# Inputs laid out by feature and weight unit, and a new order for the first eight units

## The reference

```python
def rmsnorm(x, g):
    xf = x.astype(jnp.float32)
    y = xf * lax.rsqrt(jnp.mean(xf * xf, axis=-1, keepdims=True) + EPS)
    return (y * g.astype(jnp.float32)).astype(x.dtype)
...
    for l in range(DEPTH):
        h = rmsnorm(x, norm_mix[l])
        y, S, b = mixer(h, S_in[l], buf_in[l], start_pos, lbs[l], w_in[l], w_o[l], hg_norm[l], pool_w[l], pool_scale[l])
        x = x + y
        h = rmsnorm(x, norm_ffn[l])
        if l % 2 == 0:
            x = x + swiglu(h, ffn_w_gate[j], ffn_w_up[j], ffn_w_down[j])
        else:
            x = x + moe(h, router[j], moe_w_gate[j], moe_w_up[j], moe_w_down[j])
```

## Time and profile before

| | |
|---|---|
| median of 3 runs | 991.08 us (989.86, 991.08, 997.3) |
| the profiled execution | 987.79 us, its span 986.0 us |
| mean granted TensorE clock | 0.971 |
| TensorE / VectorE / ScalarE / GpSimd busy | 93% / 71% / 58% / 17% |

### The profile page before, as it was taken

How to read it: one execution, slowest core, us unless ns; L and a number is a source line. 1 busy time by engine, 2 the same in 40 slices (tenths; PEclk the granted TensorE clock), 3 DMA queues, 4 the chain that set the end, 5 groups by cost and what they waited for, 6 DMA issues and landing times.

```text
span 986.0 us, 15383 instructions
## 1 busy us (share of the span) xinstructions
PE 917.2 (93%) x5943; PEld 843.2 (86%) x5943; DVE 697.8 (71%) x814; ACT 574.6 (58%) x711; POOL 170.3 (17%) x146
## 2 busy tenths in 40 slices
PE   0698999999999999989996999999999999999996
PEld 0598989999999999989886897888888888888886
DVE  0579947466665554797546568898989889898953
ACT  0555447554444335644544476878786868787842
POOL 0207405621121211273071000000000000000000
PEclk9999979999999999999896799999999999999999
DMA  9374303596569854632025458999999999899911
GB/s 267 89 214 129 108 1 106 150 250 186 174 200 284 217 150 135 172 113 73 28 92 172 147 176 321 414 389 352 368 366 349 376 343 394 328 407 318 394 40 45
DMA packets 171186, 217.82 MB, mean 221 GB/s; under 512 B 6908, under 2 KB 141244, under 8 KB 170986
## 3 DMA queue, kind: packets, MB, share of 16 engines
q1 hardware_dynamic: 163293, 206.25, 62.0%
q10 hardware_dynamic: 6461, 5.54, 1.9%
q0 software_dynamic: 1376, 5.27, 1.8%
HBM read 210.06 MB, written 7.43 MB: 221 GB/s over the span
## 4 chain that ended last, share of the span: by engine, by line
PE 80%; DVE 6%; ACT 3%; issue 3%; POOL 3%; DMA 3%; ACTq 2%; DVEq 0%; SPq 0%; POOLq 0%
PE bank L1565 37%; PE bank L1295 9%; PE bank L1296 9%; PE bank L1297 9%; PE bank L1539 3%; PE bank L1324 2%; PE bank L1435 2%; PE bank L1365 2%; PE bank L1614 2%; DMA sb_raw<-in_ffn_w_up_dram 1%; POOL at_state L468 1%; ACTq L501 1%; ACT sb_w_hi L512 1%; DVE at_sided L948 1%; PE bank L1574 1%
## 5 line engine op out<-in xcount | busy, mean ns | idle before, releaser
L861 DVE TENSOR_TENSOR sb_w_lo<-sb_raw,sb_w_hi 128x1024 fp32r<-128x1024 f32 (+1 forms) x116 | 163.5, 1412 | 81.0 <-ACT sb_w_hi L512 78.8
L512 ACT ACTIVATE sb_w_hi<-sb_raw 128x1024 fp32r<-128x1024 f32 (+1 forms) x116 | 126.9, 1100 | 135.3 <-PE bank L1297 116.9
L1295 PE MATMUL bank<-at_act_hi,sb_w_hi 128*128 128x264 f32 x672 | 193.9, 288 | 10.8 <-DVE sb_w_lo L861 8.1
L1565 PE MATMUL bank<-sb_w_hi,at_packed 128*128 128x512 f32 (+1 forms) x768 | 192.6, 380 | 3.0 <-DVE sb_w_lo L1073 1.6
L1296 PE MATMUL bank<-at_act_lo,sb_w_hi 128*128 128x264 f32 x672 | 191.4, 285 | 0.0
L1297 PE MATMUL bank<-at_act_hi,sb_w_lo 128*128 128x264 f32 x672 | 191.3, 285 | 0.0
L1073 DVE TENSOR_TENSOR sb_w_lo<-at_raw_e,sb_w_hi 128x1408 fp32r<-128x1408 f32 (+1 forms) x112 | 159.2, 1448 | 29.0 <-ACT sb_w_hi L723 28.9
L1073 DVE TENSOR_TENSOR sb_w_lo<-sb_raw,sb_w_hi 128x1408 fp32r<-128x1408 f32 (+1 forms) x104 | 149.9, 1472 | 21.1 <-ACT sb_w_hi L723 20.4
L1565 PEld LDWEIGHTS bank<-sb_w_hi,at_packed 128*128 128x128 f32 x768 | 141.4, 190 | 27.1 <-DVE at_packed L1087 1.7
L723 ACT ACTIVATE sb_w_hi<-at_raw_e 128x1408 fp32r<-128x1408 f32 (+1 forms) x112 | 139.4, 1245 | 42.8 <-PE bank L1565 37.2
L723 ACT ACTIVATE sb_w_hi<-sb_raw 128x1408 fp32r<-128x1408 f32 (+1 forms) x104 | 130.5, 1262 | 37.5 <-PE bank L1565 35.7
(11 more groups left out here) (258 smaller groups left out, 1428.3 us busy)
## 6 DMA issues: line engine op xcount, KB each, us to landing
sb_raw<-in_moe_w_up_dram SPq DMA_DIRECT2D x36, 704.0 KB, 7.3
at_raw_e<-in_moe_w_down_dram SPq DMA_DIRECT2D x49, 512.0 KB, 6.6
at_raw_e<-in_moe_w_gate_dram SPq DMA_DIRECT2D x35, 704.0 KB, 8.6
sb_raw<-in_w_in_dram SPq DMA_DIRECT2D x40, 512.0 KB, 4.0
sb_raw<-in_moe_w_gate_dram SPq DMA_DIRECT2D x29, 704.0 KB, 8.8
sb_raw<-in_moe_w_down_dram SPq DMA_DIRECT2D x39, 512.0 KB, 4.7
at_raw_e<-in_moe_w_up_dram SPq DMA_DIRECT2D x28, 704.0 KB, 6.0
sb_raw<-in_ffn_w_gate_dram SPq DMA_DIRECT2D x22, 512.0 KB, 4.0
```

The source lines that it names most:

```text
L512: act.activation(w_hi[s][:, 0:kts, :], raw[s][:, 0:kts, :], ACT.Copy).then_inc(hi_done, 1)
L861: dve.tensor_tensor(w_lo[s][:, 0:kts, :], raw[s][:, 0:kts, :], w_hi[s][:, 0:kts, :].bitcast(f32), ALU.subtract).then_inc(lo_done, 1)
L1295: pe.matmul(out[:, 0:T], w_hi[s][:, k, :], hi[:, c, :], start=(c == 0), stop=False)
L1565: mm = pe.matmul(bank[first_bank + p][:, 0:width], s, w[:, c0:c0 + width], start=(k == 0 and n == 0), stop=(k == last and n == 2))
```

## The change

- The inputs are rearranged before the launch (no arithmetic): x by feature, the vectors as one table of 128 rows, every dense weight by unit so that a unit is one contiguous block with 4 KB (down: 5.6 KB) per partition; state, pool map and router likewise, and the recurrent states are stored by feature and turned back afterwards. The expert weights stay as they are.
- Start: SP loads x in four pieces of two tiles, then units 1, 2, 3 (the constants between), units 4 to 7, and then the state, tables, past rows, pool map and router. ACT issues only the vector table and unit 0. No transposes.
- ACT and DVE: two tiles of x, unit 0's split, the other six tiles, units 1 and 2. TensorE's unit 0 waits per tile of `act_lo`.
- Squares on ACT (four, two tiles each), POOL adds them up to one tile in four adds, TensorE does one ones matmul after unit 2, into bank 7. The copy of the pooling state to its output is issued by POOL after these adds.
- Units 4 to 7 of `in0` use banks 4 to 7, so the first eight units wait for no read. ACT takes the root after split 4, then the lower bounds' Exp; DVE reads units 0 to 2 at step (0,2), and makes the lower bounds after the read of unit 3.

The diff, cut to its core (unmarked changes are renamed semaphores and loads that take the new arrays):

```diff
-            if name[:2] == "in":
-                w, col = a["w_in"][layer], ds(GROUPS[it] * 512 + s * 128, 128)
-            elif name[:3] == "out":
-                w, col = a["w_o"][layer], ds(it * 512 + s * 128, 128)
-            elif name[:6] == "ffn_up":
-                w, col = (a["ffn_w_gate"], a["ffn_w_up"])[s % 2][0], ds(it * 256 + (s // 2) * 128, 128)
-            else:
-                half = s % 2
-                w, col = a["ffn_w_down"][0, half * D_FF_E:(half + 1) * D_FF_E, :], ds(it * 256 + (s // 2) * 128, 128)
-            return w[:, col].rearrange("(k p) n -> p k n", p=128)
+            units = {"in": a["in_units"], "out": a["out_units"], "ffn_up": a["up_units"], "ffn_down": a["down_units"]}[name[:-1]][layer]
+            return units[ds(RING * it + s, 1)].rearrange("a p k n -> p (a k) n")
...
         def wait_x(eng, version, kt):
 
             if version == 0:
-                eng.wait_ge(x_loaded, kt + 1)
+                eng.wait_ge(x_in[kt // 2], 16)
...
+        def in_bank(layer, it, s):
+
+            return s + RING if layer == 0 and it == 1 else s
...
-            sp.dma_start(consts[:, 0:C_BEFORE], a["consts"][:, 0:C_BEFORE]).then_inc(consts_in, 16)
...
-                sp.dma_start(vec_rows[row:row + view.shape[0], :], view).then_inc(vecs_in, 16)
+            for i in range(KT // 2):
+                sp.dma_start(xT[:, 2 * i:2 * i + 2, :], a["x_cols"][:, 2 * i:2 * i + 2, :]).then_inc(x_in[i], 16)
+
+            def load_state(layer):
+                for i in range(4):
+                    sp.dma_start(state[:, 2 * i:2 * i + 2, :, :], a["state_cols"][layer, :, 2 * i:2 * i + 2, :, :]).then_inc(state_in, 16)
             for name, n0, units, kts in PASSES:
                 def load(it, s, check=True):
                     if check:
...
                     sp.dma_start(raw[s][:, 0:kts, :], unit_source(name, it, s)).then_inc(raw_full[s], 16)
                 first = 0
                 if n0 == 0:
+                    load(0, 1, check=False)
+                    sp.dma_start(consts[:, 0:C_BEFORE], a["consts"][:, 0:C_BEFORE]).then_inc(consts_in, 16)
+                    load(0, 2, check=False)
+                    load(0, 3, check=False)
                     for s in range(RING):
-                        load(0, s, check=False)
-                    first = 1
+                        load(1, s)
+                    load_state(0)
+                    sp.dma_start(consts[:, C_BEFORE:], a["consts"][:, C_BEFORE:]).then_inc(tables_in, 16)
+                    sp.dma_start(pool_past[:, :], a["state_pool"][0].rearrange("b r c -> (b r) c")).then_inc(past_in, 16)
+                    sp.dma_start(pool_w[:, :, :], a["pool_w_cols"][0]).then_inc(pool_w_in, 16)
+                    sp.dma_start(router[:, :, :], a["router_cols"]).then_inc(router_in, 16)
+                    first = 2
...
+            for n, (to, of, width, squares, sums) in enumerate(((0, 2, 2, 2, 0), (4, 6, 2, 4, 0), (0, 4, 2, 4, 2), (0, 1, 1, 4, 3))):
+                gp.wait_ge(x_squared, squares)
+                if sums:
+                    gp.wait_ge(squared, sums)
+                gp.tensor_tensor(square[:, to:to + width, :], square[:, to:to + width, :], square[:, of:of + width, :], ALU.add).then_inc(squared, 1)
+            gp.dma_start(o["new_pool_sample"][:, :, 0:POOL_BUF - 1, :], a["state_pool"][:, :, 1:POOL_BUF, :]).then_inc(shift_out, 16)
...
+                gp.dma_start(o["new_hgrn_sample"][layer], state[:, :, :, :]).then_inc(state_out, 16)
...
-            for i in range(2):
-                act.dma_start(x_rows[0:ROWS, i, :], a["x_prompt"][0, ROWS * i:ROWS * (i + 1), :]).then_inc(x_in, 16)
-            act.dma_start(x_rows[0:LAST_PROMPT, 2, :], a["x_prompt"][0, 2 * ROWS:SEQ, :]).then_inc(x_in, 16)
-            act.dma_start(x_rows[LAST_PROMPT:ROWS, 2, :], a["x_sample"][:, 0, :]).then_inc(x_in, 16)
-            act.wait_ge(x_in, 64)
-            act.dma_start(consts[:, C_BEFORE:], a["consts"][:, C_BEFORE:]).then_inc(tables_in, 16)
-            act.dma_start(pool_past[:, :], a["state_pool"][0].rearrange("b r c -> (b r) c")).then_inc(past_in, 16)
-            act.dma_start(pool_w[:, :, :], a["pool_w"][0].rearrange("g c d -> c g d")).then_inc(pool_w_in, 16)
-            for i in range(4):
-                act.dma_start(state[:, 2 * i:2 * i + 2, :, :].rearrange("k b h v -> k (b h) v"),
-                              a["state_hgrn"][0, 2 * i:2 * i + 2].rearrange("b h k v -> k (b h) v")).then_inc(state_in, 16)
-            act.dma_start(router[:, :, :], a["router"][0].rearrange("(k p) e -> p k e", p=128)).then_inc(router_in, 16)
-            act.wait_ge(lb_step, 3)
-            act.activation(lb_tmp[:, 1:3, :], lb_tmp[:, 1:3, :], ACT.Exp).then_inc(lb_exp, 1)
+            act.dma_start(vecs[:, :], a["vecs"]).then_inc(vecs_in, 16)
+            act.dma_start(raw[0][:, 0:KT, :], unit_source("in0", 0, 0)).then_inc(raw_full[0], 16)
...
                 if n0 == 0:
-                    for s in range(3):
+                    act.wait_ge(vecs_in, 16)
+                    for kt in range(2):
+                        scale_x(0, kt)
+                    split(0, 0, 0, kts, guard=False)
+                    for kt in range(2, KT):
+                        scale_x(0, kt)
+                    for s in range(1, 3):
                         split(s, 0, s, kts, guard=False)
-                    inverse_root(0)
+                        for c in range(4 * s - 4, 4 * s, 2):
+                            act.activation(square[:, c:c + 2, :], xT[:, c:c + 2, :], ACT.Square).then_inc(x_squared, 1)
...
+                    if (it, s) == (0, 1) and L == 0:
+                        inverse_root(0, 7)
+                        act.wait_ge(lb_step, 3)
+                        act.activation(lb_tmp[:, 1:3, :], lb_tmp[:, 1:3, :], ACT.Exp).then_inc(lb_exp, 1)
...
-            dve.wait_ge(vecs_turned, 1)
-            dve.tensor_copy(vecs[:, :], bank[7][:, 0:V_COLS]).then_inc(vecs_ready, 1)
-            dve.wait_ge(vecs_ready, 1)
+            dve.wait_ge(vecs_in, 16)
...
+            def lower_bounds():
+
+                dve.wait_ge(lb_exp, 1)
+                dve.tensor_tensor(top, e0, e1, ALU.add).then_inc(lb_step, 1)
...
                 if n0 == 0:
-                    for s in range(3):
+                    for kt in range(2):
+                        scale_x(0, kt)
+                    split(0, 0, kts)
+                    for kt in range(2, KT):
+                        scale_x(0, kt)
+                    for s in range(1, 3):
                         split(s, s, kts)
...
-                    dve.wait_ge(unit_used, n + 1)
-                    dve.wait_ge(rstd_done, (1, 3)[L])
-                    out = proj[:, GROUPS[it], s, :] if it < 4 else up[:, s, PAD:]
-                    dve.tensor_tensor(out, bank[s][:, 0:T], rstd[:, :], ALU.mult).then_inc(bank_read, 1)
+                    if L == 0 and it == 0 and s < 2:
+                        return
+                    for r in range(3) if L == 0 and (it, s) == (0, 2) else (s,):
+                        dve.wait_ge(unit_used, IN0[L] + 4 * it + r + 1)
+                        dve.wait_ge(rstd_done, (1, 3)[L])
+                        out = proj[:, GROUPS[it], r, :] if it < 4 else up[:, r, PAD:]
+                        dve.tensor_tensor(out, bank[in_bank(L, it, r)][:, 0:T], rstd[:, :], ALU.mult).then_inc(bank_read, 1)
+                    if L == 0 and (it, s) == (0, 3):
+                        lower_bounds()
...
-            pe.wait_ge(consts_in, 16)
-            pe.wait_ge(vecs_in, 16 * 6)
-            pe.transpose(bank[7][:, 0:V_COLS], vec_rows[:, :], ident[0:V_COLS, 0:V_COLS]).then_inc(vecs_turned, 1)
-            pe.wait_ge(x_in, 64)
-            for kt in range(KT):
-                if kt >= 4:
-                    pe.wait_ge(x_loaded, kt - 3)
-                for i, (t0, rows) in enumerate(TOKEN_TILES):
-                    mm = pe.transpose(bank[kt % 4][:, t0:t0 + rows], x_rows[0:rows, i, 128 * kt:128 * (kt + 1)], ident[0:rows, 0:rows])
-                mm.then_inc(x_turned, 1)
             def sum_squares(nth, square, b):
 
-
-                tiles = KT if nth == 0 else 1
-                for kt in range(tiles):
-                    pe.wait_ge(squared, kt + 1 if nth == 0 else SQUARED[nth + 1])
-                    mm = pe.matmul(bank[b][:, 0:T], ones, square[:, kt, :], start=(kt == 0), stop=(kt == tiles - 1))
-                mm.then_inc(summed, 1)
+                pe.wait_ge(squared, SQUARED[nth + 1])
+                pe.matmul(bank[b][:, 0:T], ones, square[:, 0, :], start=True, stop=True).then_inc(summed, 1)
...
-                        out = bank[s - half]
+                        fresh = n0 == 0 and isinstance(it, int) and it < 2
+                        out = bank[in_bank(0, it, s) if fresh else s - half]
                         pe.wait_ge(lo_done, n + 1)
-                        if half == 0 and not first:
+                        if half == 0 and not fresh:
```

(34 more changed lines are left out.)

113 lines of the change are left out of this document (52 added, 61 removed).

## The result

| | before | changed |
|---|---|---|
| shown here: median (lowest to highest) | 993.97 us (989.86 to 997.3, 4 runs) | 969.48 us (968.58 to 971.12, 4 runs) |
| ratio, 95% interval | | 0.974, 0.969 to 0.979 |
| a second set: median (lowest to highest) | 996.31 us (991.04 to 1000.12, 7 runs) | 966.11 us (964.05 to 971.22, 4 runs) |
| ratio, 95% interval | | 0.972, 0.967 to 0.977 |
| profiled execution, its span | 987.79 us, 986.0 us | 971.12 us, 969.3 us |

The kernel became 2.6% faster. The time lies 10.5 us above the forecast of 959 and 2.5 us outside its range; the second set's median, 966.11, lies 7 us above it and just inside. The direction and most of the mechanism held.

The account below looks back on a forecast made before the run. It took TensorE as the bound, with its first 36 us lost to load and work order; 27.4 + 2.9 + 1.6 = 31.9 us off 987.79 gave 955.9, plus 3.3 to the median 959; range 952 to 967.

Parts of the forecast that it names:

- Step 6: SP's queue, 3.4 MB of state and tables ahead of unit 8's load: 0 to 2 us, taken as 0.
- Step 8: Long rows for every unit load and the state's store: 1.6 us off, TensorE's weight wait between 150 and 250 us.
- Step 2: The new start: TensorE's first projection matmul at 8.7 us instead of 36.1, 27.4 us off.
- early bound: At the start, the earliest landing of unit 0's weights, 5.6 us; the latest was 7.1, and 6.35 was taken.
- Steps 3 and 4: x keeps up with unit 0; the sum of squares takes 2.9 us off TensorE, POOL's adds hidden by 0.4.
- rival C: At the start, the four pieces of x pay their start in turn: 2.4 us later, 961.6; chance 0.05.
- Step 5: Root ahead of split 5, done by 24.9; units 3 and 4 fill TensorE until 25.6; four banks cost a fraction.
- slow bound: Unit 8's load at 280 GB/s lands near 34 us, where it must be in by 32: 2 us.
- Step 7: The mixer behind unit 8 keeps its order on every engine, so the shift carries through unchanged.
- rival E: The vector chain at 80 to 110 us stays where it was; 20 of the 31.9 eaten: 979; chance 0.04.
- Rival A: TensorE waits within the first nine units, together 3 to 6 us: 962 to 965; chance 0.17.

Follow-up runs that it names:

- interleaved run: The changed kernel with the state's four loads one behind each of units 8 to 11, the smaller loads behind units 12 to 14: 963.65 us, ratio 0.9678.
- two delays: The changed kernel with SP and ACT starting after one or two memsets on POOL, about 1 us each: 967.94 and 969.31 us.
- order only: The kernel before, with the eight loads of tables, state and router issued by SP behind units 4 to 7 instead of by ACT: 990.34 us, ratio 0.9929.
- layout only: The kernel before with only the dense and projection weights laid out by unit: 990.5 us, ratio 0.9966.
- both repairs: The changed kernel with state and table loads between and behind units 8 to 15, and the state stored in 512-byte rows: 960.99 us, ratio 0.9668.
- short-row store: The changed kernel with the state stored in rows of 512 bytes again, as before: 963.22 us, ratio 0.966.
- filled pause: The kernel with both repairs, plus six unused matmuls in TensorE's 1.41 us pause behind the first four gathers: 963.28 us, ratio 0.9675.
- before again: The kernel before, unaltered, run for a second profile: 997.0 us, ratio 0.9998.

## Why the prediction was right or wrong

**Which steps failed.** Two terms of the sum were mis-sized and one cost was left out. Step 6 put 0 us on unit 8's load, and the runs show 2.3. Step 8 put nothing on what the state's longer rows do to the transfers beside them, and the runs show 1.0. And the sum stood on a median of 991.08, which later sets put at 996 to 997, more than 5 us above it. Together these are 8.4 us or a little more, and the two sets missed the forecast by 10.5 and 7.1. What is left is within what the clock moves one and the same kernel.

**Step 2, the new start: right,** 8.49 us for 8.7, but with two errors that nearly cancel. Unit 0's load was issued at 1.21 and took 4.6 us, so it landed at 5.8, near the early bound and not at the 6.35 that I took. And ACT's table load at 4.02, 1.28 us, which I hadn't named, pushed the two scalings to 5.32 and unit 0's split behind them to 6.14, 0.4 us after the landing. The order of the loads is 12.9 us of this, by the run that changes it alone; the rest, which no run takes apart, I put mostly to the transposes and the scalings that no longer stand in a row.

**Steps 3 and 4: right.** Unit 1 follows unit 0 without a pause, and the scalings of x never wait for one of its pieces, so rival C fell. POOL's adds ended 0.40 us late instead of 0.4 early: the last three took 5.70 us in all, 1.9 each and not 1.4, between the two rows I had the earlier trace rows. That it was so little is luck: ACT's squares were done at 13.7 and not at 14.8. The sum itself is 0.68 us of busy time instead of 3.72.

**Step 5: right on when, too low on the banks.** DVE's first read ran at 24.73; unit 5's split ended at 24.82 for 24.9. The banks were priced at a fraction of a us. The wait without them is 2.13 us, and the value transposes came 1.5 to 1.7 us later, with some low clock in it.

**Step 6 is the term that failed.** The working bracketed the outcome: bounds of 29 and 34 for unit 8, needed by 32. It landed at 33.63, almost at the slow bound. I took the fast side, "since all these rows but the smallest are 4 KB or more". The row of 24 to 34 us shows 363 GB/s, not 424, the one from 17 us to the landing 348. And more was in flight than the bytes I counted (3.4 MB, POOL's 0.46 and the unit's own 0.5): 5.8 MB moved in that time. The loads of units 6 and 7 landed only at 17.83 and 20.68, and those of units 9 to 11 were issued behind unit 8's before it was in. The wait seen on TensorE is 1.25 us, but ACT and DVE had lost 5 us of their lead, and the vector chain behind them paid too: 2.3 us in all, by the interleaved run. The slow bound's 2 us would have been right to 0.3. The rule of the Trainium skill weighed at that step, "DMA: Bandwidth & Descriptors", Issuing engines are not separate DMA queues, has loads of all queues run on the same engines, so that by it the bytes would have been as late on ACT's queue. No run here has them there with the new start, so it stays untested.

**Step 7: right,** by the two delays; rival E fell. Rival A is what happened, at the adds and at unit 8, with waits of 0.40 and 1.25 us. The one at unit 8 was worth the 2.3; with the 0.40 that is still less than the 3 to 6 that A gave.

**Step 8: half right.** The pause of rows 11 is gone, and across the dense layer the shift grows by 1.9 us in both profiles (27.9 to 29.9, 29.6 to 31.5). That is the layout of the units by itself: from the dense layer's sum of squares to layer 1's the kernel before takes 196.3 us, and 194.3 or 194.4 with the layout alone as well as with the store back in short rows. So the store in long rows, which I had counted in, frees nothing there. It costs: the store of h beside it is slower, and TensorE waits 1.0 us more. ACT's waits for the experts' gate weights in the gathers' stretch are 6.2 us in all for 5.2; that stays when the store is undone (6.3), is not there with the layout alone (5.1) or the order alone (5.0), and its cause is open.

**The base: mis-sized, and the largest part of the miss.** I put the median of the kernel before at 991.08, from three runs. In the later sets it is 996.31 (7 runs), 996.75 (19) and 996.15 (17), and its runs go from 987.21 to 1001.27. Of the 10.5 us by which I missed, about 5 are this: with 31.9 off 996.5 the forecast would have been 964.6. The difference of the medians is 24.5 us in the first set and 30.2 in the second.

**What moves the runs is the clock.** Twice (1 - granted clock), summed over a profile, is the time at 1.2 GHz:

| | whole span | from 12 us before the first gather matmul to 40 after it | span |
|---|---|---|---|
| before | 58.1 us | 27.3 us | 986.0 us |
| before, second profile | 75.2 | 27.3 | 997.4 |
| changed | 83.2 | 37.5 | 969.3 |
| changed, second profile | 68.1 | 37.5 | 962.4 |
| order only | 96.8 | 37.5 | 990.7 |
| layout only | 64.8 | 27.3 | 987.3 |
| both repairs | 65.7 | 27.3 | 958.5 |

Between the two profiles of one kernel, 17.2 us more at 1.2 GHz go with 11.4 us of span, and 15.1 with 6.9: 0.46 to 0.66 us for each. In one stage it is cleaner. From layer 0's value transposes to the dense layer's sum of squares five profiles took 64.0, 65.6, 67.2, 68.8 and 70.5 us, with the clock low for 10.2, 13.7, 17.1, 20.5 and 23.9 (changed second, before, interleaved, before second, short-row store): 0.47 us for each. If I put it at a half, as an estimate, and take it off, before is left with 956.9 and 959.7, the changed kernel with 927.7 and 928.3. The mean difference is 30.3 us. The sum, 31.9, less the 2.3 and the 1.0 is 28.6. So with the clock set aside the steps hold to within 2 us, which is no better than the estimate of a half.

The first profiles of both kernels show where the rest went: their spans differ by 16.7 us, which is 27.9 gained up to the value transposes and 1.9 in the dense layer, less 4.9 in layer 1's mixer (clock low 6.8 us longer), 6.5 in the router and gathers, and 1.7 behind them (8 us longer). The granted clock does not tell all: in both kernels the first matmuls follow each other at 0.22 us and not at 0.12, for 4 us, while it reads 1.00.

The second column is where the 6 us of the changed kernel's profiles went. The stretches of 18 us that begin 12 us after the first gather matmul, of before, changed, order only and both repairs:

```profile
546.10:564.10 18.00, 18.00 (x104) 16.54 (x105) 10.04 (x9) 7.97 (x11) 0.00 (x0) 0.82 0.50 165
```

```profile
522.16:540.16 18.00, 18.00 (x76) 16.66 (x77) 7.03 (x6) 4.96 (x8) 0.00 (x0) 0.56 0.44 147
```

```profile
543.80:561.80 18.00, 18.00 (x76) 16.62 (x77) 7.07 (x7) 5.05 (x8) 0.00 (x0) 0.57 0.42 141
```

```profile
517.23:535.23 18.00, 18.00 (x103) 16.54 (x104) 9.84 (x9) 7.77 (x11) 0.00 (x0) 0.81 0.51 163
```

TensorE is busy throughout in all four, and gets through 104 and 103 instructions at a mean clock of 0.82 and 0.81, but 76 at 0.56 and 0.57. In the first ten profiles each of the old order had the short dip and each of the new order the long one, and I took it for an effect of the change. The order-only kernel has the long one with the old layouts, and the one with both repairs the short one with the new. So the change does not force either. What decides it is open; that the new order makes the long dip likelier isn't excluded by these 14 profiles, and nor that the long-row store does: all seven profiles with that store have the long one. One thing in the records goes with the outcome. In the four profiles with the short dip the clock had fallen 8.4 to 9.0 us before the first gather matmul, in the nine with the long one 9.3 to 10.5 us before it. The kernel with the filled pause fell 9.5 us before it and came back early even so, where the one with the short-row store, at 9.5 too, stayed low for 37.5 us. So the filled pause may have worked on the clock, which no run here tests further.

## What to carry to other kernels

A block of loads that nobody needs soon still delays the weight unit issued behind it, and moving the block as a whole moves the wait; put its pieces between the units, one each. Count in its bytes what is already in flight. Price a longer-row transfer also for what runs beside it. Anchor a forecast of 3% on more than three runs where the kernel's own runs differ by 1.4%, and look at how long the clock was low in the profile that you lean on.

## What the runs showed that I had not expected

- A 2 MB store in long rows slows a store of 1.08 MB beside it more than the same store in rows of 512 bytes: 11.95 us to its landing against 9.7, and TensorE's wait behind it 3.7 us against 2.7.
- The clock's low time in runs of one unchanged kernel differs by 17 us (58.1 and 75.2), and its times by 14 us (987.21 to 1001.27).
- In one stretch with the same work on TensorE the clock came back 14.9 to 15.5 us after the first gather matmul in four profiles without the filled pause (before, before again, layout only, both repairs), and 24.9 to 28.0 us after it in nine; in the one with the filled pause 14.4, and soon down again.
